# Four buffers for conditioning weights, sums transposed into a PSUM bank, and a layer norm split over two engines

## The chip, the core and the metric

The kernel runs on one core of one Trainium2 chip. The metric is device time in microseconds: the median of several executions. A profiled execution is one more run, whose trace is read below. Engines are PE (TensorE: matmuls and transposes; PEld is its weight load), DVE (VectorE), ACT (ScalarE), POOL and SP (the queue from which the weights are loaded).

## What is computed

Two blocks on x of 256 rows by 2048 columns, all in float32: a block with a gated delta rule, block attention and a feed-forward net, and then two conditioned layers. Of the second part this matters here:

```python
c_act = jax.nn.silu(c)
for l in range(2):
    mod = c_act @ w_mod[l] + b_mod[l]          # 1 x 2048 by 2048 x 6144
    shift, scale, gate = jnp.split(mod, 3, axis=-1)
    h = x * (1.0 + scale[:, None]) + shift[:, None]
    if l == 0:
        y = diff_attention(h, ...)             # products v2 k2 q2 g2, then o2
    else:
        mod = c_act @ w_mod_kv + b_mod_kv      # 1 x 2048 by 2048 x 4096
        # keys and values of the normalized x (products v3 k3), queries and gate (q3 g3), o3
        y = forgetting_attention(h, ...)
    x = layer_norm(DN_ALPHA * x + gate[:, None] * y, ln_g[l], ln_b[l])
```

The vectors `mod` depend on `c` alone, so they can be computed at any earlier time.

## The kernel before

Rows of x are the 128 partitions, in two halves `th`. Each product reads its weights in units of 256 x 512 (512 KB). A unit goes through a ring of four slots: SP loads it into `raw` (L467), ACT casts it to `w_hi` (L1281, `split`), DVE subtracts to get `w_lo` (L1908, `split`), and PE multiplies three ways: `w_hi` by the high operand, `w_lo` by the high one, `w_hi` by the low one (L661 to L663, or L686 to L688 in the transposed form). Each engine's program is written out in the order in which it runs, and the semaphores `w_landed`, `hi_done`, `lo_done` and `w_used` tie them. ACT and DVE work four units ahead: at unit j they prepare unit j + 4, ACT waits until unit j is used (`w_used`), and SP's load of unit j waits for `lo_done` of unit j - 4 (L465). A list `between(j)` hangs other work on the units.

The conditioning vectors are computed beside the products `qkv`, `spill`, `w_out`, `ffn`, `down`, `v2`, `k2` and `q2`, in 32 chunks of 512 columns. A chunk is 16 steps, one per unit: SP loads 128 x 512 of `w_mod` (256 KB) into `gemv_w[:, k % 2]` and DVE adds it, times one entry of `c_act`, to `gemv_acc` (L1924, L1927). SP issues step j - 5 right behind the weight load of unit j; the load of step k waits until step k - 2 has been added (`gemv_step`, L490), and what follows in SP's queue waits with it. After the last step DVE transposes `gemv_acc` in 32 x 32 blocks into `gemv_t` (L1931) and reduces that to `gemv_sums` (L1935); at unit 5 of the next chunk PE adds over partitions into bank `MODB` (L696), and at unit 7 ACT copies and stores the result (L1306, L1309).

Between `qkv` and `spill` lies a gate computation: DVE forms the argument of a softplus (L2096 to L2102), ACT takes Exp (L1425) and Ln (L1426), and PE, after two units of `spill` that carry nothing else and a third, waits for `softplus_log` before it goes on (L794). Its own next steps are sums of squares (L802).

The first layer's end, `o2`, is followed at once by `v3`, whose operand is the normalized x, and nothing else is left for PE between them. The last two units of `o2` run the upper rows first and then the lower (`rows_apart`, L637 to L639). DVE drains each half (L2520, L2524), takes moments (L2529, L2552), ACT takes a dummy Sqrt, which loads the table, and the root (L1786, L1333), DVE the reciprocal (L2587) and then, chunk by chunk, both halves of `normalized` (L2601), each raising `ln_out`. PE turns chunk c when `ln_out` has reached 2(c + 1) (`turn_normed`, L1222; the transposes are L604). From the turned blocks `even_block` on DVE (L2459) and `odd_block` on ACT (L1723) make the modulated operand, ACT casts it to `s_hi` (L1712), DVE subtracts `s_lo` (L2466), and PE's unit j of `v3` needs blocks j (`cut_by`). `v3` starts with the first two chunks turned and turns the third and fourth behind its units 0 and 1.

Of the kernel before, what the change touches and what calls it, by code (L numbers as in the profile page):

```python
# [18 lines left out]
F32 = mybir.dt.float32  # L19
F32R = mybir.dt.float32r  # L20
ALU = mybir.AluOpType
# [4 lines left out]
P = 128  # L26
# [13 lines left out]
SQ = 32  # L40
RING = 4
RMS_EPS = 1e-6
EPS = 1e-5
# [70 lines left out]
def block_kernel(nc, x, norm_mix_w, w_in, conv_w, a_log, dt_bias, gdn_o_norm_w, q_norm_w, k_norm_w,  # L114
# [5 lines left out]
    with ctx:  # L120
# [14 lines left out]
        keep = place("keep", [P, KEEP_W], F32)  # L135
        cols = place("cols", [P, 3 * P], F32)
        modc = place("modc", [P, P], F32)
        small = place("small", [P, 464], F32)
        stage = place("stage", [P, 2, HALVES, COLS], F32)
        f_first = place("f_first", [P, H3, P], F32, at[0])  # L140
        gemv_w = place("gemv_w", [P, 2, COLS], F32)
        gemv_acc = place("gemv_acc", [P, COLS], F32)
        gemv_t = place("gemv_t", [P, COLS], F32)
        gemv_sums = place("gemv_sums", [P, COLS // SQ], F32)
# [103 lines left out]
        def h_stage(q):  # L248
# [9 lines left out]


        SS, RR, GCOL, BB, EGL, NEGA, ALOG, DTB = 0, 32, 64, 128, 144, 176, 177, 178  # L260
        LN_STATS, LN_MOMENTS = 336, 322
        E6, E5, QNS, BFC, MX, SUM, RCP, LAM, RELB, FCOL, CACT = (
            179, 180, 181, 182, 192, 256, 320, 384, 400, 416, 448)
        c_act = small[:, CACT:CACT + KD]
# [82 lines left out]
        x_in = (sem("x_in0"), sem("x_in1"))  # L347
        gemv_landed = (sem("gemv_landed0"), sem("gemv_landed1"))
        gemv_cut = sem("gemv_cut")
# [105 lines left out]
        def _(sp):  # L455
# [23 lines left out]
            def load_gemv(pr, i, j, w, col):  # L479

                if without_mod(pr, i):
                    return
                part = pr.units // pr.mods
                m, k = j // part, j % part
                if k >= KD:
                    return
                n = mod_base(pr, i) + m
                if not (isinstance(i, int) and (n + i * pr.mods) * KD + k < 2):

                    sp.wait_ge(gemv_step, i * (pr.mods * KD) + (n * KD + k - 1))  # L490
                sp.dma_start(gemv_w[:, k % 2], w[k * P:(k + 1) * P, ds(col + m * COLS, COLS)]).then_inc(gemv_landed[k % 2], 16)

# [100 lines left out]
        def _(pe):  # L593
# [627 lines left out]
            def turn_normed(c):  # L1221
                pe.wait_ge(signal("ln_out"), HALVES * (c + 1))  # L1222

                turn_x(products["v3"], c, lambda q: (signal("h_odd"), c) if q else (signal("h_block"), 8 + c))

            turn_normed(0)
            turn_normed(1)
# [43 lines left out]
        def _(act):  # L1271
# [495 lines left out]
            def layer_tail(name, p, layer, extra=None):  # L1767
# [5 lines left out]
                if layer:  # L1773
                    ln_weights(layer)

                for i in range(pr.bodies):
                    def between(j, i=i):
                        if i == 0 and j == 3:
                            outputs_high(pr, p, 3)
                        if extra:  # L1780
                            extra(i, j)


                    body(name, i, nothing, between, finish=(lambda: None) if i == pr.bodies - 1 else None)

                own.link(act.activation(ln_tmp[layer][:, 0, D - 1:D], sm(E5, 1), ACT.Sqrt, bias=sm(E5, 1)))  # L1786
                if layer == 0:
                    act.wait_ge(signal("moments"), HALVES)
                    root(0, small[:, LN_MOMENTS + 1:LN_MOMENTS + 2 * HALVES:2], sm(RR, HALVES), 1.0, E5, "root_ln")
                    return  # L1790
                for th in range(HALVES):
                    act.wait_ge(signal("moments"), HALVES + th + 1)
                    root(0, sm(LN_MOMENTS + 2 * th + 1), sm(RR + th), 1.0, E5, "root_ln")

# [66 lines left out]

            layer_tail("o2", "d", 0, forget_weights)
            odd_block(1)
            for q in range(2):
                v3_operand(q)
            for i in range(2):
                def between(j, i=i):
                    if i == 0 and j < 3:
                        v3_operand(2 * j + 2)
                        v3_operand(2 * j + 3)  # L1870
# [30 lines left out]
        def _(dve):  # L1901
# [8 lines left out]
            def gemv(pr, i, j):  # L1910
# [7 lines left out]
                n = mod_base(pr, i) + m  # L1918
                c_k, w_k = c_act[:, k:k + 1], gemv_w[:, k % 2]
                dve.wait_ge(gemv_landed[k % 2], i * (pr.mods * 8 * KD) + (n * 8 * KD + 16 * (k // 2 + 1)))  # L1920
                if k == 0:
# [7 lines left out]
                if k == KD - 1:  # L1929
                    dve.wait_ge(gemv_step, i * (pr.mods * KD) + (n * KD + KD))  # L1930
                    dve.transpose(gemv_t[:], gemv_acc[:]).then_inc(gemv_cut, 1)  # L1931
                    dve.wait_ge(gemv_cut, i * (pr.mods * 2) + (2 * n + 1))
                    if not (isinstance(i, int) and i * pr.mods + n == 0):
                        dve.wait_ge(mod_stored, i * (pr.mods * 16) + 16 * n)
                    dve.tensor_reduce(gemv_sums[:], gemv_t[:].rearrange("p (b c) -> p b c", c=SQ), AX.X, ALU.add).then_inc(  # L1935
                        gemv_cut, 1)
# [579 lines left out]
            def residual_drain(pr, i, x, ths=range(HALVES)):  # L2516
# [5 lines left out]
                for th in ths:  # L2522
                    c = xs[:, th, ds(i * (2 * COLS) + x * COLS, COLS)]
                    dve.scalar_tensor_tensor(out=c, in0=c, scalar=ALPHA, in1=stage[:, x, th], op0=ALU.mult,  # L2524
                                             op1=ALU.add).then_inc(signal("x_mixed"), 1)
                layer, chunk = int(pr is products["o3"]), 2 * i + x
                for th in ths:
                    dve.wait_ge(signal("x_mixed"), 8 * layer + 2 * chunk + th + 1)
                    own.inc(dve.bn_stats(sm(LN_STATS + 24 * th + 6 * chunk, 6), xs[:, th, chunk * COLS:(chunk + 1) * COLS]))  # L2529
# [7 lines left out]
            def layer_tail(name, p, layer, extra=None):  # L2537
# [26 lines left out]
                def last_of_x():  # L2564
# [4 lines left out]
                    if layer:  # L2569
                        dve.wait_ge(signal("moments"), HALVES + 1)  # L2570
                        dve.wait_ge(signal("ln_in"), 64)
                        own.inc(centred(0, slice(0, D)))
                        dve.wait_ge(signal("root_ln"), 2)
                        own.link(dve.reciprocal(sm(RR), sm(RR)))
# [8 lines left out]

                if layer == 0:
                    dve.wait_ge(signal("moments"), HALVES)
                    dve.wait_ge(signal("root_ln"), 1)
                    own.link(dve.reciprocal(sm(RR, HALVES), sm(RR, HALVES)))  # L2587
                    return
                finished(0, parts[1])
                dve.wait_ge(signal("moments"), 2 * HALVES)  # L2590
                own.inc(centred(1, parts[0]))
                dve.wait_ge(signal("root_ln"), 3)
                own.link(dve.reciprocal(sm(RR + 1), sm(RR + 1)))
# [242 lines left out]
```

## Time and profile before

| | us |
|---|---|
| median of 3 runs | 2598.83 (2596.96 to 2603.57) |
| profiled execution | 2601.48 |
| its span, first to last instruction | 2599.7 |
| PE busy | 2554.0 |
| DVE busy | 1803.6 |
| ACT busy | 1154.6 |
| mean granted clock of PE | 0.995 of full speed |

All times in the rows below count from the start of the span. PE is called busy from the start of a matmul to its modelled end. The granted clock is the share of 2.4 GHz that the chip let PE run at; it has two levels, 1.00 and 0.50.

### The profile page before, as it was taken

How to read it: one execution, taken by the hardware profiler on the slowest of the kernel's cores; microseconds unless marked ns; L12 is line 12 of the kernel's file. 1: busy time of each engine (PE TensorE's matmuls, PEld its weight loads, DVE VectorE, ACT ScalarE, POOL GpSimd, SP SyncE). 2: the span in 40 equal slices, each digit the busy share in tenths (PEclk: the TensorE clock that was granted, in tenths of full speed). 3: DMA queues.
4: the chain of work that ended last, by engine and by line, in shares of the span. 5: the costliest groups of instructions: out<-in, count | busy, mean ns of one | idle time of the engine just before them, and what ended most of it. 6: DMA issues, size and time to landing. Idle time of an engine off the chain costs nothing.

```text
span 2599.7 us, 38429 instructions
## 1 busy us (share of the span) xinstructions
PE 2554.0 (98%) x14550; PEld 2156.5 (83%) x14550; DVE 1803.6 (69%) x2342; ACT 1154.6 (44%) x1475; POOL 0.2 (0%) x4
## 2 busy tenths in 40 slices
PE   8999999999999999999999999999999999999998
PEld 8977878778888888888888888899987778999886
DVE  6897676776667777777776666776786665545756
ACT  5454333445544544444443334333486344334642
POOL 0000000000000000000000000000000000000000
PEclk9999999999999999999999999999999999999999
DMA  6777676776768888888887777888845546675464
GB/s 212 247 236 247 210 249 216 255 255 211 251 227 271 270 276 276 270 272 278 277 276 250 251 253 258 280 275 275 257 138 189 186 159 181 185 230 178 137 215 143
DMA packets 317949, 605.74 MB, mean 233 GB/s; under 512 B 27742, under 2 KB 31844, under 8 KB 316140
## 3 DMA queue, kind: packets, MB, share of 16 engines
q1 hardware_dynamic: 301628, 571.59, 68.3%
q10 hardware_dynamic: 16176, 32.15, 3.6%
q8 instruction: 99, 1.62, 0.2%
q14 instruction: 46, 0.38, 0.0%
HBM read 593.03 MB, written 10.62 MB: 232 GB/s over the span
## 4 chain that ended last, share of the span: by engine, by line
PE 90%; DVE 4%; DMA 2%; ACT 2%; issue 2%; SPq 0%; ACTq 0%; DVEq 0%
PE bank L661 22%; PE bank L663 22%; PE bank L662 22%; PE bank L688 5%; PE bank L686 5%; PE bank L687 5%; DMA gemv_w<-in_w_mod 2%; PE bank L604 2%; PE bank L787 1%; DVE gemv_acc L1927 1%; DVE w_lo L1908 1%; DVE conv_out L2056 1%; ACT w_hi L1281 1%; PE bank L1120 1%; PE bank L813 0%
## 5 line engine op out<-in xcount | busy, mean ns | idle before, releaser
L1908 DVE TENSOR_TENSOR w_lo<-raw,w_hi 128x1024 fp32r<-128x1024 f32 x820 | 1001.7, 1223 | 725.9 <-ACT w_hi L1281 723.9
L1281 ACT CAST w_hi<-raw 128x1024 fp32r<-128x1024 f32 x820 | 859.3, 1049 | 1347.1 <-PE bank L663 1001.7
L661 PE MATMUL bank<-w_hi,u_hi 128*128 128x512 f32 x1216 | 491.9, 404 | 6.3 <-issue 3.8
L663 PE MATMUL bank<-w_hi,u_lo 128*128 128x512 f32 x1216 | 481.2, 396 | 0.0
L662 PE MATMUL bank<-w_lo,u_hi 128*128 128x512 f32 x1216 | 480.9, 395 | 0.0
L1927 DVE SCALAR_TENSOR_TENSOR gemv_acc<-gemv_w,small,gemv_acc 128x512 f32<-128x512 f32 x480 | 357.9, 746 | 23.2 <-DMA gemv_w<-in_w_mod 21.9
L661 PE MATMUL bank<-w_hi,s_hi 128*128 128x512 f32 x744 | 300.9, 404 | 1.3 <-DVE w_lo L1908 1.2
L663 PE MATMUL bank<-w_hi,s_lo 128*128 128x512 f32 x744 | 294.2, 395 | 0.0
L662 PE MATMUL bank<-w_lo,s_hi 128*128 128x512 f32 x744 | 294.2, 395 | 0.0
L688 PE MATMUL bank<-s_hi,w_lo 128*128 128x256 f32 x1024 | 290.1, 283 | 0.0
L687 PE MATMUL bank<-s_lo,w_hi 128*128 128x256 f32 x1024 | 289.5, 283 | 0.0
L686 PE MATMUL bank<-s_hi,w_hi 128*128 128x256 f32 x1024 | 288.7, 282 | 0.0
L661 PEld LDWEIGHTS bank<-w_hi,u_hi 128*128 128x128 f32 x1216 | 229.7, 189 | 65.6 <-issue 10.2
L663 PEld LDWEIGHTS bank<-w_hi,u_lo 128*128 128x128 f32 x1216 | 229.7, 189 | 53.9
L662 PEld LDWEIGHTS bank<-w_lo,u_hi 128*128 128x128 f32 x1216 | 230.0, 189 | 49.3
L686 PEld LDWEIGHTS bank<-s_hi,w_hi 128*128 128x128 f32 x1024 | 193.7, 189 | 0.3
L688 PEld LDWEIGHTS bank<-s_hi,w_lo 128*128 128x128 f32 x1024 | 193.1, 189 | 0.0
L687 PEld LDWEIGHTS bank<-s_lo,w_hi 128*128 128x128 f32 x1024 | 192.7, 188 | 0.1
L663 PEld LDWEIGHTS bank<-w_hi,s_lo 128*128 128x128 f32 x744 | 140.4, 189 | 33.0
L661 PEld LDWEIGHTS bank<-w_hi,s_hi 128*128 128x128 f32 x744 | 140.6, 189 | 32.7 <-DVE w_lo L1908 1.6
L662 PEld LDWEIGHTS bank<-w_lo,s_hi 128*128 128x128 f32 x744 | 140.7, 189 | 30.6
L661 PE MATMUL bank<-w_hi,hid_hi 128*128 128x512 f32 x352 | 139.8, 397 | 0.0
(362 smaller groups left out, 2882.6 us busy)
## 6 DMA issues: line engine op xcount, KB each, us to landing
gemv_w<-in_w_mod SPq DMA_DIRECT2D x384, 256.0 KB, 3.2
raw<-in_w_in SPq DMA_DIRECT2D x176, 512.0 KB, 4.5
raw<-in_a_w_in SPq DMA_DIRECT2D x128, 512.0 KB, 4.5
raw<-in_w_ffn_gate SPq DMA_DIRECT2D x88, 512.0 KB, 4.6
raw<-in_w_ffn_up SPq DMA_DIRECT2D x88, 512.0 KB, 4.4
raw<-in_w_ffn_down SPq DMA_DIRECT2D x88, 512.0 KB, 4.3
gemv_w<-in_kv_w_mod SPq DMA_DIRECT2D x128, 256.0 KB, 3.5
raw<-in_kv_w SPq DMA_DIRECT2D x64, 512.0 KB, 3.7
```

The source lines that it names most:

```text
L604: ins = pe.transpose(b[:, f * T + th * P:f * T + (th + 1) * P], src(f, th), ident)
L661: pe.matmul(o, xh, w_hi[:, s, t], start=(k == 0), stop=False)
L662: pe.matmul(o, xh, w_lo[:, s, t], start=False, stop=False)
L663: ins = pe.matmul(o, xl, w_hi[:, s, t], start=False, stop=(k == 2 * units - 1))
L686: pe.matmul(o, wh, hi[:, k], start=(k == 0 and f % 2 == 0), stop=False)
L687: pe.matmul(o, wh, lo[:, k], start=False, stop=False)
L688: ins = pe.matmul(o, wl, hi[:, k], start=False, stop=(k == 2 * half - 1 and f % 2 == 1))
L787: ins = pe.matmul(dst[rr, n:n + CHUNK], lhs[rr, th, h], rhs[rr, th, h], start=True, stop=True)
L1120: pe.matmul(b[:, P:3 * P], queries_of[p][:, a, P:T], k_t[:, a, 0:T], start=True, stop=True).then_inc(signal(p + "_scores"), 1)
L1281: act.copy(w_hi[:, s], raw[:, s]).then_inc(hi_done, 1)
L1908: dve.tensor_tensor(w_lo[:, s], raw[:, s], w_hi[:, s].bitcast(F32), ALU.subtract).then_inc(lo_done, 1)
L1927: dve.scalar_tensor_tensor(out=gemv_acc[:], in0=w_k, scalar=c_k, in1=gemv_acc[:], op0=ALU.mult, op1=ALU.add).then_inc(gemv_step, 1)
```

## The change

Three edits are made together.

1. `gemv_w` has four buffers in place of two, with a semaphore for each; the load of step k waits for step k - 4. Space comes from `gemv_t`, which goes, and from shorter `cols` and `small`.
2. DVE transposes `gemv_acc` into `bank[MODB]` and reduces from there. It waits for the store of the chunk before (`mod_stored`) ahead of the transpose, no longer between transpose and reduce.
3. In the layer norm after `o2`, ACT normalizes the upper half (`upper_normalized`: Identity with scale and a bias `SHIFTED` that DVE computes as minus mean times reciprocal root), and DVE the lower half. ACT's dummy Sqrt moves ahead of its last two casts, and the root of the upper half ahead of the last. PE runs 16 matmuls of 512 columns on the operand of the layer before, into `bank[MODB]`, between `o2` and the first transposes; nothing reads them. A semaphore `x_rows` takes over what `x_mixed` counted and, for DVE's half, what `ln_out` counted.

```diff
-        cols = place("cols", [P, 3 * P], F32)
+        cols = place("cols", [P, LN_B + KD], F32)
-        small = place("small", [P, 464], F32)
+        small = place("small", [P, 448], F32)
-        gemv_w = place("gemv_w", [P, 2, COLS], F32)
+        gemv_w = place("gemv_w", [P, GEMV_RING, COLS], F32)
-        gemv_t = place("gemv_t", [P, COLS], F32)
...
# SP, load_gemv
-                if not (isinstance(i, int) and (n + i * pr.mods) * KD + k < 2):
-                    sp.wait_ge(gemv_step, i * (pr.mods * KD) + (n * KD + k - 1))
-                sp.dma_start(gemv_w[:, k % 2], w[k * P:(k + 1) * P, ds(col + m * COLS, COLS)]).then_inc(gemv_landed[k % 2], 16)
+                if not (isinstance(i, int) and (n + i * pr.mods) * KD + k < GEMV_RING):
+                    sp.wait_ge(gemv_step, i * (pr.mods * KD) + (n * KD + k - (GEMV_RING - 1)))
+                sp.dma_start(gemv_w[:, k % GEMV_RING], w[k * P:(k + 1) * P, ds(col + m * COLS, COLS)]).then_inc(gemv_landed[k % GEMV_RING], 16)
...
# PE, before v3
             def turn_normed(c):
-                pe.wait_ge(signal("ln_out"), HALVES * (c + 1))
+                pe.wait_ge(signal("ln_out"), c + 1)
+                pe.wait_ge(signal("x_rows"), 8 + 1 + c + 1)
...
+            for n in range(16):
+                pe.matmul(bank[MODB][:], s_hi[:, n, 0:P], s_hi[:, n // 2 * 2:n // 2 * 2 + 2], start=True, stop=True)
             turn_normed(0)
...
# ACT, layer_tail
+                def first_root():
+                    own.link(act.activation(ln_tmp[layer][:, 0, D - 1:D], sm(E5, 1), ACT.Sqrt, bias=sm(E5, 1)))
+
+                def root_ln(th):
+                    act.wait_ge(signal("moments"), HALVES * layer + th + 1)
+                    root(0, sm(LN_MOMENTS + 2 * th + 1), sm(RR + th), 1.0, E5, "root_ln")
...
-                    body(name, i, nothing, between, finish=(lambda: None) if i == pr.bodies - 1 else None)
-
-                own.link(act.activation(ln_tmp[layer][:, 0, D - 1:D], sm(E5, 1), ACT.Sqrt, bias=sm(E5, 1)))
-                if layer == 0:
-                    act.wait_ge(signal("moments"), HALVES)
-                    root(0, small[:, LN_MOMENTS + 1:LN_MOMENTS + 2 * HALVES:2], sm(RR, HALVES), 1.0, E5, "root_ln")
-                    return
-                for th in range(HALVES):
-                    act.wait_ge(signal("moments"), HALVES + th + 1)
-                    root(0, sm(LN_MOMENTS + 2 * th + 1), sm(RR + th), 1.0, E5, "root_ln")
+                        if layer == 0 and i == pr.bodies - 1 and j == pr.units - 1:
+                            root_ln(0)
+                    body(name, i, nothing, between, finish=first_root if i == pr.bodies - 1 else None)
+
+                if layer:
+                    root_ln(0)
+                root_ln(1)
+
+            def upper_normalized(c):
+                act.wait_ge(signal("x_rows"), 8 + 1)
+                part = xs[:, 0, c * COLS:(c + 1) * COLS]
+                act.activation(part, part, ACT.Identity, scale=sm(RR), bias=sm(SHIFTED)).then_inc(signal("ln_out"), 1)
...
             layer_tail("o2", "d", 0, forget_weights)
+            upper_normalized(0)
+            upper_normalized(1)
             odd_block(1)
...
                 def between(j, i=i):
+                    if i == 0 and j < 2:
+                        upper_normalized(2 + j)
...
# DVE, gemv
-                    dve.transpose(gemv_t[:], gemv_acc[:]).then_inc(gemv_cut, 1)
-                    dve.wait_ge(gemv_cut, i * (pr.mods * 2) + (2 * n + 1))
                     if not (isinstance(i, int) and i * pr.mods + n == 0):
                         dve.wait_ge(mod_stored, i * (pr.mods * 16) + 16 * n)
-                    dve.tensor_reduce(gemv_sums[:], gemv_t[:].rearrange("p (b c) -> p b c", c=SQ), AX.X, ALU.add).then_inc(
+                    dve.transpose(bank[MODB][:], gemv_acc[:]).then_inc(gemv_cut, 1)
+                    dve.wait_ge(gemv_cut, i * (pr.mods * 2) + (2 * n + 1))
+                    dve.tensor_reduce(gemv_sums[:], bank[MODB][:].rearrange("p (b c) -> p b c", c=SQ), AX.X, ALU.add).then_inc(
                         gemv_cut, 1)
...
# DVE, layer_tail and normalized
-                    dve.wait_ge(signal("moments"), HALVES)
-                    dve.wait_ge(signal("root_ln"), 1)
-                    own.link(dve.reciprocal(sm(RR, HALVES), sm(RR, HALVES)))
+                    dve.wait_ge(signal("root_ln"), 1)
+                    own.link(dve.reciprocal(sm(RR), sm(RR)))
+                    dve.wait_ge(signal("moments"), HALVES)
+                    dve.scalar_tensor_tensor(out=sm(SHIFTED), in0=sm(LN_MOMENTS), scalar=-1.0, in1=sm(RR), op0=ALU.mult,
+                                             op1=ALU.mult).then_inc(signal("x_rows"), 1)
+                    dve.wait_ge(signal("root_ln"), 2)
+                    own.link(dve.reciprocal(sm(RR + 1), sm(RR + 1)))
                     return
...
             def normalized(c):
                 part = slice(c * COLS, (c + 1) * COLS)
-                for th in range(HALVES):
-                    dve.tensor_scalar(xs[:, th, part], xs[:, th, part], sm(LN_MOMENTS + 2 * th), sm(RR + th), ALU.subtract,
-                                      ALU.mult).then_inc(signal("ln_out"), 1)
+                dve.tensor_scalar(xs[:, 1, part], xs[:, 1, part], sm(LN_MOMENTS + 2), sm(RR + 1), ALU.subtract,
+                                  ALU.mult).then_inc(signal("x_rows"), 1)
```

## Rows read from the trace of the kernel before

**Rows 1.** The page: busy us by engine, share of the span, instructions.

```profile
PE 2554.0 (98%) x14550; PEld 2156.5 (83%) x14550; DVE 1803.6 (69%) x2342; ACT 1154.6 (44%) x1475; POOL 0.2 (0%) x4
```

**Rows 2.** Windows of 20 us: length, busy by engine, PE clock, DMA share, GB/s.

```profile
160.00:180.00 20.00, 15.29 (x71) 12.55 (x71) 17.52 (x26) 12.64 (x17) 0.00 (x0) 0.91 0.74 241
520.00:540.00 20.00, 19.94 (x90) 15.97 (x90) 16.75 (x17) 7.83 (x7) 0.00 (x0) 1.00 0.95 329
540.00:560.00 20.00, 17.61 (x73) 13.73 (x72) 18.77 (x18) 11.30 (x16) 0.00 (x0) 0.91 0.76 240
2080.00:2100.00 20.00, 14.64 (x62) 11.54 (x63) 14.21 (x26) 10.24 (x18) 0.00 (x0) 0.74 0.27 79
```

**Rows 3.** Waits of PE, 60 to 182 us: us in total, times, longest.

```profile
PE bank L686 <- DVE w_lo L1908: 1.8, 3, 0.9
```

**Rows 4.** Waits of DVE for conditioning weights: 100-180, 165-181, 500-540 us.

```profile
DVE gemv_acc L1927 <- DMA gemv_w<-in_w_mod: 7.5, 7, 1.9
DVE gemv_acc L1927 <- DMA gemv_w<-in_w_mod: 2.1, 2, 1.7
DVE gemv_acc L1927 <- DMA gemv_w<-in_w_mod: 4.2, 4, 2.5
```

**Rows 5.** The chain that ended last, near 525 us: start, us, what.

```profile
524.90 7.55 DMA gemv_w<-in_w_mod
```

**Rows 6.** Timeline, 160 to 181 us: start, us, engine, line, what, [idle before, releaser].

```profile
166.13 1.05 ACT L1281 CAST w_hi<-raw 128x1024 fp32r<-128x1024 f32 x1 [3.03 <-DMA raw<-in_w_in]
169.13 1.22 DVE L1908 TENSOR_TENSOR w_lo<-raw,w_hi 128x1024 fp32r<-128x1024 f32 x1
171.28 0.39 PE L663 MATMUL bank<-w_hi,u_lo 128*128 128x512 f32 x1
171.98 0.39 PE L663 MATMUL bank<-w_hi,u_lo 128*128 128x512 f32 x1
173.52 0.42 DVE L2102 TENSOR_TENSOR gates<-gates 8x256 f32<-8x256 f32 x1
175.70 0.41 ACT L1426 ACTIVATE gates<-gates 8x256 f32<-8x256 f32 x1
176.22 0.64 PE L661 MATMUL bank<-w_hi,u_hi 128*128 128x512 f32 x1 [3.85 <-issue]
179.64 0.46 PE L663 MATMUL bank<-w_hi,u_lo 128*128 128x512 f32 x1
```

**Rows 7.** Timeline, 545 to 549 us.

```profile
546.75 2.35 DVE L1908 TENSOR_TENSOR w_lo<-raw,w_hi 128x1024 fp32r<-128x1024 f32 x2
548.01 0.50 PE L661 MATMUL bank<-w_hi,u_hi 128*128 128x512 f32 x1 [2.39 <-DVE w_lo L1908]
```

**Rows 8.** Timeline of the layer norm and the start of v3, 2080 to 2097 us.

```profile
2081.64 0.30 ACT L1333 ACTIVATE small<-small 128x2 f32<-128x2 f32 x1
2082.24 1.92 DVE L2601 TENSOR_SCALAR xs<-xs,small 128x512 f32<-128x512 f32 x4
2083.34 1.94 PE L604 MATMUL bank<-keep,xs 128*128 128x128 f32 x8 [4.48 <-issue]
2087.68 0.77 PE L661 MATMUL bank<-w_hi,s_hi 128*128 128x512 f32 x1
2096.70 0.63 PE L604 MATMUL bank<-keep,xs 128*128 128x128 f32 x4 [0.71 <-DVE stage L2459]
```

**Rows 9.** Groups by form: count, busy us, mean ns of one, idle before.

```profile
L1931 DVE STREAM_TRANSPOSE gemv_t<-gemv_acc 128x512 f32<-128x512 f32 x32 | 22.8, 712 | 1.1
L2208 DVE TENSOR_REDUCE small<-work 128x1 f32<-128x256 f32 x32 | 13.1, 409 | 0.0
L2208 DVE TENSOR_REDUCE small<-bank 128x1 f32<-128x256 f32 x8 | 3.3, 413 | 0.0
L1712 ACT CAST s_hi<-stage 128x512 fp32r<-128x512 f32 x8 | 4.8, 619 | 8.3 <-DVE stage L2459 8.2
L1723 ACT ACTIVATE stage<-bank,modc 128x256 f32<-128x256 f32 x8 | 4.1, 557 | 3.4 <-PE bank L604 3.4
```

More of the change, by code:

```diff
@@ L41 @@
 RING = 4
+GEMV_RING = 4
 RMS_EPS = 1e-6
@@ L257, in block_kernel @@
         operand_of = {"d": (s_hi, s_lo), "f": (s2_hi, s2_lo)}
+        SHIFTED = 410
         SS, RR, GCOL, BB, EGL, NEGA, ALOG, DTB = 0, 32, 64, 128, 144, 176, 177, 178
@@ L262, in block_kernel @@
         E6, E5, QNS, BFC, MX, SUM, RCP, LAM, RELB, FCOL, CACT = (
-            179, 180, 181, 182, 192, 256, 320, 384, 400, 416, 448)
+            179, 180, 181, 182, 192, 256, 320, 183, 384, 416, 392)
         c_act = small[:, CACT:CACT + KD]
@@ L347, in block_kernel @@
         x_in = (sem("x_in0"), sem("x_in1"))
-        gemv_landed = (sem("gemv_landed0"), sem("gemv_landed1"))
+        gemv_landed = [sem(f"gemv_landed{s}") for s in range(GEMV_RING)]
         gemv_cut = sem("gemv_cut")
@@ L1918, in gemv @@
                 n = mod_base(pr, i) + m
-                c_k, w_k = c_act[:, k:k + 1], gemv_w[:, k % 2]
-                dve.wait_ge(gemv_landed[k % 2], i * (pr.mods * 8 * KD) + (n * 8 * KD + 16 * (k // 2 + 1)))
+                c_k, w_k = c_act[:, k:k + 1], gemv_w[:, k % GEMV_RING]
+                dve.wait_ge(gemv_landed[k % GEMV_RING], i * (pr.mods * 4 * KD) + (n * 4 * KD + 16 * (k // GEMV_RING + 1)))
                 if k == 0:
@@ L2524, in residual_drain @@
                     dve.scalar_tensor_tensor(out=c, in0=c, scalar=ALPHA, in1=stage[:, x, th], op0=ALU.mult,
-                                             op1=ALU.add).then_inc(signal("x_mixed"), 1)
+                                             op1=ALU.add).then_inc(signal("x_rows"), 1)
                 layer, chunk = int(pr is products["o3"]), 2 * i + x
                 for th in ths:
-                    dve.wait_ge(signal("x_mixed"), 8 * layer + 2 * chunk + th + 1)
+                    dve.wait_ge(signal("x_rows"), 13 * layer + 2 * chunk + th + 1)
                     own.inc(dve.bn_stats(sm(LN_STATS + 24 * th + 6 * chunk, 6), xs[:, th, chunk * COLS:(chunk + 1) * COLS]))
@@ L2572, in last_of_x @@
                         own.inc(centred(0, slice(0, D)))
-                        dve.wait_ge(signal("root_ln"), 2)
+                        dve.wait_ge(signal("root_ln"), 3)
                         own.link(dve.reciprocal(sm(RR), sm(RR)))
@@ L2591, in layer_tail @@
                 own.inc(centred(1, parts[0]))
-                dve.wait_ge(signal("root_ln"), 3)
+                dve.wait_ge(signal("root_ln"), 4)
                 own.link(dve.reciprocal(sm(RR + 1), sm(RR + 1)))
```

## The prediction

> **What bounds the kernel now.** The first view is busy time by engine: TensorE (PE) works 2554.0 of 2599.7 us [rows 1]. Only the 45.7 us in which it stands still, and the stretches in which its clock is low, can be won; work saved on another engine counts for nothing unless PE waits for it. The second view, PE and clock in slices of 20 us, shows where that is: 4.7 us idle from 160 to 180 and 2.4 from 540 to 560, both with a mean clock of 0.91, and 5.4 from 2080 to 2100 with 0.74 [rows 2]. The rest lies at the start and the end of the span and in pieces of about 1 us that no edit touches, but for three waits for the low half of the weights, 1.8 us in all, between 60 and 182 [rows 3].
>
> Then each hole is read. VectorE (DVE) waited 7.5 us for conditioning weights between 100 and 180, 2.1 of that after 165, and 4.2 between 500 and 540 [rows 4]. The chain that ended last runs through such loads: a 256 KB load that took 7.55 us stands on it [rows 5]. The reason is in the code: with two buffers the load for step k waits until step k-2 has been added up, and the sync queue (SP) holds the next weight load behind that wait.
>
> At 172 us PE has finished three units and waits for softplus_log. The order is visible: DVE's last w_lo split at 169.13, then gemv, transpose, reduce, the gate arithmetic with its last step at 173.52, then ScalarE (ACT) with Exp, a table load and Ln, done at 176.11; PE starts again at 176.22 after 3.85 idle, and its next 8 intervals take 3.42 us, 0.43 each, against 0.23 before [rows 6]. That is the 1.2 GHz level in place of 2.4. At 548.01 PE had waited 2.39 us for a split that DVE began at 546.75 [rows 7]. In the third hole PE stops at 2078.87, the layer norm runs alone on DVE, and PE's transposes start at 2083.34, after 4.48 us, at 1.2 GHz (8 in 1.94 us); the first matmul of v3 starts at 2087.68, and the transposes of the last chunk wait again until 2096.70 [rows 8].
>
> **The change, part by part.**
> *Four buffers, first hole.* SP's wait for the load of step k now asks for step k-4, which is done before the split that frees the raw buffer next in the queue. The conditioning load leaves about one unit (2.8 us) sooner and the weight load behind it about one gemv sooner, so DVE's waits of up to 2.5 us go. How early can DVE be? At least 2.1 (the waits after 165). At most 5.9: the w_lo of a unit needs its w_hi, which needs the unit four before it used; three units of 12 matmuls at 0.233 ended at 172.37, so that one was used at 164.0 and, with the three small waits gone, at 162.2, so w_hi ends at 163.2 (1.05 long) where DVE started at 169.13 [rows 3, 6]. I take the middle, 4.0. The gate arithmetic then ends at 169.9 instead of 173.9; ACT's 2.2 us behind it stay; softplus_log comes at 172.1. PE reaches the wait 1.8 earlier, at 170.6, stands 1.5 us, and goes on 4.0 us earlier than before. After waits of up to 0.9 [rows 3] the clock stayed (the 0.09 that the slice from 160 lost is 3.4 us at half speed, all of it after 176), after 2.39 and more it fell [rows 2, 7]; I count 1.5 with the former, so the slow matmuls, 8 x (0.4275 - 0.233) = 1.56 us, are saved too. Term: 5.6. Bounds: 2.1 (least shift, clock falls) and 7.2 (no idle left: 1.8 + 3.85 + 1.56). DVE waits for less and nothing new is queued ahead of it; what is late next is ACT's Exp, table load and Ln.
>
> *Second hole.* The gemv waits in 500 to 540 are 4.2 us and the missing time is 2.39, so the split comes in time and PE keeps its clock: 2.39 + 1.56 = 4.0. Bounds: 4.0 and 0, if the weight loads, in a stretch whose DMA engines are 95% busy [rows 2], arrive no sooner. I take 4.0, since the waits exceed what is missing by 1.8 us.
>
> *Elsewhere* DVE's waits for these loads end no wait of PE: its own are those of rows 3 and 6 to 8 and the pieces of 1 us. 0.
>
> *Transpose into a bank.* A transpose of 128x512 into SBUF takes 0.711 us; none into a bank is in the trace. The nearest row is the reduce of 128x256, 0.413 from a bank and 0.409 from SBUF [rows 9]. So 0 to 0.01 per chunk on DVE, in both directions; bound from above 0.1, the whole being covered by DVE's slack except for four chunks at the two holes: 0 taken, 0.4 at most. The wait for mod_stored moves ahead of the transpose; that store is issued at unit 7 of a group and the transpose stands at unit 15, some 22 us later, so nobody waits; behind it would stand the next split.
> The Trainium skill (Perfetto Trace Analysis, section Optimizing Scalar/DVE Operations) gives DVE about 60 ns of access time on SBUF and 125 ns on a bank. By it transpose and reduce would cost 0.13 us more per chunk, as an estimate 0.5 us for the four chunks that matter, and the sum would be 11.2. The two reduce rows show 4 ns, and I go by them.
>
> *Layer norm on two engines, 16 matmuls on PE.* Before, DVE makes four passes in 1.92 us from 2082.24, and PE starts after two of them [rows 8]. Now ACT takes the upper half's pass while DVE takes the lower. ACT's 128x512 pass with scale and bias is not in the trace: 0.62 for a plain one is the lower bound, and 0.56 for 256 columns with scale and bias [rows 9], doubled, 1.1 the upper. I take 0.75, nearer to the row of the same size. The dummy Sqrt and its table load move from just ahead of the root, which ran from 2081.64 [rows 8], to ahead of ACT's last two w_hi casts, where ACT waits for PE anyway; I count 0.2 for that. ACT's pass needs one small DVE step more (the shift) but not the lower half's reciprocal, 0.2 again. So it starts about 0.4 before 2082.24 and both halves of chunk 0 are ready at about 2082.6, against 2083.3. The 16 matmuls (16 x 0.233 = 3.7 from 2078.9) end at 2082.6, as that chunk gets ready, and cost PE nothing; the clock is then high for the transposes (8 in about 1.0 instead of 1.94). First matmul of v3: before 2087.68, now about 2086.3 (0.7 from the norm, 0.6 from faster transposes). It runs full speed, but the end of the stretch is set by DVE and ACT: unit 0 used, w_hi, w_lo, one normalizing pass (0.5 shorter than two), the even block, then the transposes that waited until 2096.70. This moves from 2096.70 to about 2094.5. Term: 2.1. Bounds: 2.4, and 1.0 if ACT's pass takes 1.1, three times in its queue ahead of a copy that DVE waits for. If the clock falls all the same in the gaps left between transposes and unit 0, unit 0 ends 1.6 later, which that second wait swallows but for 0.3.
> The same page and section of the Trainium skill says that where DVE has a faster mode an operation is quicker there, which speaks against moving a pass to ACT. The trace agrees: 0.48 a pass on DVE (four in 1.92) against 0.62 at least on ACT [rows 8, 9]. By it one chunk would be ready after 0.96 on DVE alone, after 0.75 on both: only 0.2 us of this term come from the second engine.
>
> Sum: 5.6 + 4.0 + 2.1 = 11.7. The profiled execution took 2601.48 us (span 2599.7 and 1.8 around it): 2589.8. The median before, 2598.83, is 2.65 lower, perhaps because a clock that fell here doesn't fall in every run; then less is to be won. From the median 11.7 gives 2587.1. I say **2588.0**.
>
> **Rivals.**
> *The weight loads become the wait.* ACT waited 3.03 us at 166.13 for a raw weight load [rows 6]; if these loads land no sooner, DVE waits for w_hi instead of gemv_w. Gain 2.1 in the first hole, 0 in the second, 2.1 in the layer norm: 2594.6. For it: the 95% in rows 2. Against: the raw loads leave sooner too.
> *It moves nothing.* The holes are filled by other waits at once (softplus through ACT, sq_b through ACT) and ACT's passes eat the layer norm's gain: 2598. Against: the named waits are longer than what follows them.
> *Slower: the loads overtake.* In every stretch with conditioning work a unit needs 768 KB in its 12 matmuls, 2.8 us: 281 GB/s. Two more 256 KB loads in flight take their share ahead of raw weights. If this makes a unit's data take more than the 2.81 us that PE needs for it, PE waits in each of 480 units; at 0.02 us a unit that is 9.6 us with no gain: 2608. Against: 329 GB/s were moved in 520 to 540 [rows 2].
>
> **How the numbers follow.** The forecast, with its terms near 5.6, 4.0 and 2.1, gets 0.69 (2584.5 to 2591); raw loads 0.22 (2594.6); nothing 0.05 (2598); slower 0.04 (2608). The range of 8 in 10 reaches from all upper bounds (13.6 off the median, 2585.2, less 1 for the spread) into the raw-load rival: 2584 to 2595. About 0.3%, 7.8 us, is what a measurement of this kernel can tell from no change. Below 2591.0 lie the forecast and little else: faster 0.69, within 0.27, slower 0.04.
>
> **What would show it.** Right: no DVE wait for gemv_w over 0.3 us in 100 to 180 and 500 to 540; PE's wait for softplus under 1.6 us and clock 1.00 in both; 16 matmuls from 2079 on end before the transposes start, and those take about 1.0 us for 8; the last chunk's transposes come about 15.6 us after o2's last matmul instead of 17.8. Wrong: a wait of DVE for w_hi with ACT waiting for raw loads of the same length, PE idle at the softplus gate of 3 us or more, a transpose over 0.8 us, or an ACT pass over 1 us.

## The result and the profile after

The changed kernel takes 2603.2 us (median of 14 runs, 2600.61 to 2606.96), the kernel before on the same chip 2599.85 us: a ratio of 1.0015, 95% interval 1.0008 to 1.0022. It is slower by a hair, where 2588.0 us was forecast. The profiled execution took 2603.11 us, its span is 2601.3 us.

The page after, busy us by engine, as in [rows 1]:

```profile
PE 2567.8 (99%) x14566; PEld 2159.7 (83%) x14566; DVE 1799.9 (69%) x2340; ACT 1157.8 (45%) x1480; POOL 0.2 (0%) x4
```

PE stood still for 2601.3 - 2567.8 = 33.5 us, against 45.7 before: 12.2 us less idle time. But PE was *busy* for 13.8 us more. The 16 extra matmuls are 3.8 of that; the other 10.0 come although the matmuls behind the three holes no longer run at the low clock.

Windows of 20 us after, with the columns of [rows 2]:

```profile
160.00:180.00 20.00, 19.88 (x94) 14.48 (x93) 18.88 (x31) 17.03 (x22) 0.00 (x0) 1.00 0.78 257
540.00:560.00 20.00, 20.00 (x94) 16.38 (x95) 17.08 (x16) 11.13 (x15) 0.00 (x0) 1.00 0.81 254
2080.00:2100.00 20.00, 16.83 (x86) 12.86 (x85) 15.20 (x27) 12.50 (x20) 0.00 (x0) 1.00 0.28 79
2460.00:2480.00 20.00, 18.12 (x93) 15.05 (x92) 11.06 (x26) 12.41 (x23) 0.00 (x0) 0.91 0.41 124
```

The three holes read as intended. At 160 PE works 19.88 us instead of 15.29 and at 540 all 20.00 instead of 17.61, both with the clock at 1.00. At the layer norm, 2080 to 2100, it is 16.83 instead of 14.64 (3.8 of it the extra matmuls) with the clock at 1.00 instead of 0.74. One clock fall is new, near 2470, where PE waits 1.88 us for ACT; the kernel before has a wait of 1.9 us at this place, and its clock stays at 1.00.

DVE's waits for conditioning weights, 100 to 180 and 500 to 540 us, as in [rows 4]: in total, times, longest:

```profile
DVE gemv_acc L1947 <- DMA gemv_w<-in_w_mod: 0.3, 1, 0.3
DVE gemv_acc L1947 <- DMA gemv_w<-in_w_mod: 1.1, 1, 1.1
```

From 7.5 to 0.3 us, and from 4.2 to 1.1. The end of the gate computation, start and length as in [rows 6]:

```profile
168.25 0.42 DVE L2122 TENSOR_TENSOR gates<-gates 8x256 f32<-8x256 f32 x1
170.43 0.41 ACT L1430 ACTIVATE gates<-gates 8x256 f32<-8x256 f32 x1
```

DVE's last gate step begins at 168.25, 5.3 us before its counterpart in [rows 6], and Ln is done at 170.84. PE has finished its three units at 170.83 and goes on at 170.94, so it hardly stops for it any more. The layer norm after, against [rows 8]:

```profile
2079.70 3.81 PE L1229 MATMUL bank<-s_hi 128*128 128x512 f32 x16
2082.08 0.26 DVE L2572 BATCH_NORM_AGGREGATE small<-small 128x2 f32<-128x24 f32 x1
2082.38 0.29 ACT L1337 ACTIVATE small<-small 128x1 f32<-128x1 f32 x1 [1.37 <-DVE small L2572]
2082.64 1.52 ACT L1809 ACTIVATE xs<-xs,small 128x512 f32<-128x512 f32 x2
2082.90 1.00 DVE L2624 TENSOR_SCALAR xs<-xs,small 128x512 f32<-128x512 f32 x2
2083.55 1.06 PE L605 MATMUL bank<-keep,xs 128*128 128x128 f32 x8
2087.05 0.47 PE L662 MATMUL bank<-w_hi,s_hi 128*128 128x512 f32 x1 [0.62 <-issue]
2094.94 0.63 PE L605 MATMUL bank<-keep,xs 128*128 128x128 f32 x4 [0.85 <-DVE stage L2479]
```

PE's 16 matmuls end at 2083.51, both engines' first passes (ACT's two take 1.52 us, DVE's two 1.00) are through by then, and 8 transposes take 1.06 us instead of 1.94. The groups that bear on [rows 9], with the same columns: the transpose and the reduce, now in a bank, and ACT's normalizing pass, which had no row before (first line: the reduce of the kernel before, from SBUF):

```profile
L1935 DVE TENSOR_REDUCE gemv_sums<-gemv_t 128x16 f32<-128x512 f32 x32 | 22.0, 686 | 2.2
L1953 DVE STREAM_TRANSPOSE bank<-gemv_acc 128x512 f32<-128x512 f32 x32 | 23.3, 727 | 2.3
L1955 DVE TENSOR_REDUCE gemv_sums<-bank 128x16 f32<-128x512 f32 x32 | 22.1, 691 | 1.1
L1809 ACT ACTIVATE xs<-xs,small 128x512 f32<-128x512 f32 x4 | 3.2, 812 | 0.0
```

So the named waits are gone but for small remainders. Where did some 15 us go, 11.7 that were forecast and 3.35 by which the kernel is slower? To a place that none of these views shows. Windows of PE alone in three long stretches without any hole: length, busy (its instructions), clock, DMA share, GB/s. First the kernel before, then the changed kernel. The first window lies in `ffn` (512 columns a matmul), the other two in `k2`/`q2` and `k3`/`q3` (256 columns):

```profile
900.00:1300.00 400.00, 400.00 (x1760) 1.00 0.85 275
1720.00:1820.00 100.00, 100.00 (x843) 1.00 0.86 276
2220.00:2320.00 100.00, 100.00 (x835) 1.00 0.68 213
```

```profile
900.00:1300.00 400.00, 400.00 (x1748) 1.00 0.86 273
1720.00:1820.00 100.00, 100.00 (x834) 1.00 0.87 273
2220.00:2320.00 100.00, 100.00 (x835) 1.00 0.69 215
```

PE is busy without a gap and at full clock in both, yet it gets through 1748 matmuls in 400 us instead of 1760, and 834 instead of 843 in 100 us. (The counts take in short ones too: of the 1760, 64 are transposes and 18 are sums of conditioning chunks. So 400 us over the count is less than the spacing of the long ones.) Loads are the same (275 and 273 GB/s). From the starts in the trace, consecutive matmuls of equal width stand 234.3 ns apart in `ffn` where it was 232.5, and 120.0 in `k2` where it was 118.7; in `k3` both have 120.0. Lining up the same matmul in both traces, the changed kernel loses 0.2 us in every 18 us of `qkv`, `k2` and `q2` and 0.24 in every 34 us of a 512-column stage. The whole account, in us: this slow drift +15.2; `qkv` and the gate (100 to 170) -8.0; the second hole -4.3; the layer norm -2.7; the clock fall ahead of `o3` near 2470 +1.6; the start +0.4. That is +2.2; the span shows 1.6 of it, since PE's first instruction came 0.6 earlier.

### The profile page after: what moved, and what is told of

It is laid out like the page before. It is cut to its first block, busy times and chain, and to the rows that moved or that the text cites. A ratio compares the mean times of both kernels' runs of the same rounds, so it can differ in the third digit from the quotient of the medians.

```text
span 2601.3 us, 38411 instructions
## 1 busy us (share of the span) xinstructions
PE 2567.8 (99%) x14566; PEld 2159.7 (83%) x14566; DVE 1799.9 (69%) x2340; ACT 1157.8 (45%) x1480; POOL 0.2 (0%) x4
## 4 chain that ended last, share of the span: by engine, by line
PE 95%; DVE 2%; ACT 2%; issue 1%; DMA 1%; ACTq 0%; SPq 0%; DVEq 0%
PE bank L662 23%; PE bank L664 22%; PE bank L663 22%; PE bank L689 7%; PE bank L687 7%; PE bank L688 6%; PE bank L605 1%; PE bank L788 1%; ACT w_hi L1285 1%; PE bank L1121 1%; DVE w_lo L1928 0%; DMA gemv_w<-in_w_mod 0%; PE bank L814 0%; PE bank L1130 0%; PE bank L803 0%
## 5 line engine op out<-in xcount | busy, mean ns | idle before, releaser
L662 PEld LDWEIGHTS bank<-w_hi,u_hi 128*128 128x128 f32 x1216 | 228.9, 188 | 60.6 <-issue 6.1
```

The source lines that it names most:

```text
L662: pe.matmul(o, xh, w_hi[:, s, t], start=(k == 0), stop=False)
```

## The experiments

What could slow a PE that never waits? Theory A: the addresses. The change makes some tiles shorter and others longer, and so moves all operands (`u_hi`, `s_hi` and the rest of the region behind `region`) from byte 104192 to 105952 of a partition, while `w_hi` stays at 32896 (`w_lo` lies 16384 behind it). The distance, operands' byte minus weights' byte, so goes from 71296 to 73056; divided by 256 these leave 128 and 96, which is what "distance modulo 256" means below. Rival B: what the change does beside PE (loads that are earlier and denser, DVE's transposes into a bank) disturbs PE.

### e1 to e4: addresses alone

e1, the changed kernel, 32 bytes lower from the staging on:

```diff
-        SHIFTED = 410
+        SHIFTED = 188
-            179, 180, 181, 182, 192, 256, 320, 183, 384, 416, 392)
+            179, 180, 181, 182, 192, 256, 320, 183, 384, 408, 392)
-        small = place("small", [P, 448], F32)
+        small = place("small", [P, 440], F32)
```

> The changed kernel with its small-vector tile 32 bytes shorter, so that everything placed behind it (staging, conditioning weights, and the region with the operands u and s) lies 32 bytes lower; nothing else differs. In the changed kernel those addresses are odd multiples of 32 bytes, here multiples of 64, as in the kernel before. Theory A (the start address of PE's operands sets how closely its matmuls follow one another: 234.3 ns for 512 columns and 120.0 ns for 256 in the changed kernel, 232.4 and 118.7 in the kernel before): the old pace returns, the 15 us that the slower pace adds along the kernel go, and the holes stay closed: 2588 us, ratio about 0.995. Rival B (the earlier and denser conditioning loads, or VectorE's transposes into the bank, slow PE): nothing moves, 2603 us, ratio 1.0015, and 234.3 and 120.0 ns stay.

2590.27 us, ratio 0.9969 [0.9959, 0.9978]. The matmuls stand 233.3 ns apart in `ffn` and 117.8 in the 256-column stages, so the pace changed, though not to that of the kernel before. The windows of e1, as above:

```profile
900.00:1300.00 400.00, 400.00 (x1754) 1.00 0.87 272
1720.00:1820.00 100.00, 100.00 (x849) 1.00 0.87 277
2220.00:2320.00 100.00, 100.00 (x851) 1.00 0.70 219
```

e2, the kernel before with 32 bytes more, and e3, with 64:

```diff
-        cols = place("cols", [P, 3 * P], F32)
+        cols = place("cols", [P, 3 * P + 8], F32)      # e2
+        cols = place("cols", [P, 3 * P + 16], F32)     # e3
```

> The kernel before with 32 bytes of padding in the column tile, ahead of the small vectors, the staging, the conditioning weights and the operands; no instruction differs. Theory A: the pace becomes that of the changed kernel (234.3 and 120.0 ns), with all holes still there: about 2600 + 15 = 2615 us, ratio 1.006. Rival B: 2600 us, ratio 1.000, the pace stays 232.4 and 118.7 ns.

2603.06 us, ratio 1.0013 [1.0004, 1.0022]: slower, but not by 15 us. 233.4 ns in `ffn`, 117.3 to 118.7 by turns for 256 columns.

> The kernel before with 64 bytes of padding at the same place. Theory A with a grain of 64 bytes: 2600 us, ratio 1.000, pace 232.4 and 118.7 ns. Theory A with a coarser grain (128 bytes or more): slower, up to 2615 us. Rival C (any shift at all disturbs the pace, by the distance of the operands from the weights or by chance): slower, like the shift of 32 bytes. Rival B: 2600 us.

2564.38 us, ratio 0.9867 [0.9852, 0.9882]. Nothing but 64 unused bytes makes the kernel before 1.3% faster, three times what the change was to bring. The windows of e3:

```profile
900.00:1300.00 400.00, 400.00 (x1789) 1.00 0.86 279
1720.00:1820.00 100.00, 100.00 (x881) 1.00 0.90 290
2220.00:2320.00 100.00, 100.00 (x851) 1.00 0.68 218
```

1789 matmuls where there were 1760, and 881 where there were 843: 228.9 and 113.4 ns; in `k3`/`q3` it is 117.8.

e4, the changed kernel with staging and conditioning buffers moved as in e1 but the operand region put back:

```diff
(the edits of e1, and)
+        at[0] += 32
         region = at[0]
```

> The changed kernel with the staging and the conditioning buffers 32 bytes lower, on multiples of 64, and 32 bytes of padding behind them, so that the operand region stays where the changed kernel has it. Theory A, by the operands of the matmuls: nothing moves, 2603 us, ratio 1.0015, 234.3 and 120.0 ns. Theory A', by the buffers that VectorE, ScalarE and the DMAs write beside PE (staging, conditioning weights): 2588 us. Rival B: 2603 us.

2604.21 us, ratio 1.0019 [1.0010, 1.0028], and the changed kernel's pace to a tenth of a ns in every stage:

```profile
900.00:1300.00 400.00, 400.00 (x1747) 1.00 0.87 272
1720.00:1820.00 100.00, 100.00 (x834) 1.00 0.86 272
```

So it is the address of the operand region, and not that of the buffers which DVE, ACT and the loads write. Rival B falls with e1 to e4: the pace changes in kernels whose instructions are the same one for one, and does not change where only the other buffers move. That the grain would be 64 bytes was wrong: 32 and 64 bytes give two different new paces.

### e5 to e8: own address or distance to the weights?

e5 moves every tile of the kernel before by 64 bytes, weights included; e8 moves the weights and keeps the operands; e6 puts the changed kernel's operands at another address with e3's distance; e7 pads 128 bytes.

```diff
-        at = [16512]
+        at = [16512 + 64]                                             # e5
-        gemv_row = place("gemv_row", [P, SQ], F32)
+        gemv_row = modc[:, 96:96 + SQ]                                # e6, with the edits of e1
+        cols = place("cols", [P, 3 * P + 32], F32)                    # e7
+        at[0] += 64                                                   # e8, ahead of w_hi
+        cols = place("cols", [P, 3 * P - 16], F32)                    # e8
```

> The kernel before with its first tile, and so every tile, 64 bytes higher: the operands u and s lie where the kernel with 64 bytes of padding has them, but the weights w_hi and w_lo move along, so the distance between operands and weights is that of the kernel before. Theory A1 (the pace goes by the operands' own address): 2564 us and 228.9 ns for a 512-column matmul in ffn, as with 64 bytes of padding. Theory A2 (it goes by the distance between operands and weights): 2599 us, 232.4 ns.

2598.26 us, ratio 0.9998 [0.9989, 1.0008], and the pace of the kernel before in every stage (matmuls begun in `ffn` and in `k2`/`q2`):

```profile
900.00:1300.00 400.00, 400.00 (x1760) 1.00 0.85 275
1720.00:1820.00 100.00, 100.00 (x843) 1.00 0.86 276
```

> The changed kernel with its operand region 160 bytes lower, at byte 105792 (the small-vector tile 32 bytes shorter, the conditioning row kept in unused columns of the modulation tile). Modulo 256 the operands then lie at 64, and 192 from the weights, as in the kernel before with 64 bytes of padding. Theory A with a grain of 256 bytes (A1 and A2 alike): that kernel's pace (228.9 ns in ffn) with the changed kernel's closed holes: 2564 - 12 = 2552 us, ratio about 0.982. Theory A3 (the pace goes by the whole address, or by chance): no reason for that pace; somewhere between 2588 and 2603 us.

2553.17 us, ratio 0.9819 [0.9806, 0.9832], at the pace of e3:

```profile
900.00:1300.00 400.00, 400.00 (x1789) 1.00 0.88 279
1720.00:1820.00 100.00, 100.00 (x882) 1.00 0.90 289
```

Its first hole is not closed in the profiled execution, which was the longest of the five (2557.81): PE comes to the gate sooner, waits 2.2 us for Ln, and its clock falls (columns of [rows 2]):

```profile
160.00:180.00 20.00, 17.82 (x75) 13.45 (x73) 19.11 (x30) 14.15 (x18) 0.00 (x0) 0.91 0.82 271
```

> The kernel before with 128 bytes of padding in the column tile. Theory A with a grain of 128 bytes: as the kernel before, 2599 us and 232.4 ns in ffn. With a grain of 256 bytes: a pace of its own, between 228.9 and 234.3 ns in ffn, 2564 to 2615 us. Rival B (contention by loads and VectorE): 2599 us.

2566.88 us, ratio 0.9881 [0.9866, 0.9897]. A pace of its own, 227.0 ns for 512 columns but 120.0 for 256:

```profile
900.00:1300.00 400.00, 400.00 (x1805) 1.00 0.86 281
1720.00:1820.00 100.00, 100.00 (x833) 1.00 0.86 273
```

> The kernel before with w_hi, w_lo, xs and the constants 64 bytes higher and the column tile 64 bytes shorter, so that the operand region stays at its address and the distance to the weights is 64 bytes less (64 modulo 256, as in the changed kernel with 32 bytes less). Theory A1 (the operands' own address): 2599 us, 232.4 ns in ffn. Theory A2 (the distance): 233.3 ns in ffn and 117.8 ns for 256 columns, about 2600 us in all, as these two shifts nearly cancel over the kernel.

2600.24 us, ratio 1.0000 [0.9991, 1.0009], at 233.3 and 117.8 ns, which is e1's pace stage by stage:

```profile
900.00:1300.00 400.00, 400.00 (x1755) 1.00 0.85 273
1720.00:1820.00 100.00, 100.00 (x849) 1.00 0.87 279
```

The four agree on theory A2: what counts is the distance between operands and weights, modulo 256 bytes. e5 keeps it and keeps the pace although every address moved. e8 changes it to that of e1 and gets e1's pace with other addresses. e6 has e3's distance at an address 1536 bytes away, and e3's pace. The full distances of e1 and e8 differ by 1792, which is a multiple of 256 but not of 512, so the pace repeats with 256 bytes. No run has the kernel before at distance 96, where the changed kernel stands; at 64 (e1, e8) and at 192 (e3, e6) the kernels with and without the change have the same pace.

### e11 and e12: the two distances left

The edit is that of e2 and e3, with `+ 40` (160 bytes) in e11 and `+ 24` (96 bytes) in e12.

> The kernel before with 160 bytes of padding in the column tile: operands 32 from the weights modulo 256, a distance not measured yet. Distances so far: 0 gives 227.0 ns for 512 columns and 119.9 for 256; 64 gives 233.3 and 117.8; 96 gives 234.3 and 120.0; 128 gives 232.4 and 118.7; 160 gives 233.4 and 117.8; 192 gives 228.9 and 113.4 to 117.7. If the slow distances lie together (64 to 160) and the quick ones around 0: between 227 and 233 ns, 2564 to 2600 us. Chance by distance: anything in 2564 to 2615 us.

2595.40 us, ratio 0.9987 [0.9977, 0.9996]; 233.3 ns, and for 256 columns 116.7 or 117.8 by turns.

> The kernel before with 96 bytes of padding in the column tile: operands 224 from the weights modulo 256, between the two quick distances 192 (228.9 ns) and 0 (227.0 ns). If the quick distances lie together: 227 to 229 ns in ffn, 2560 to 2570 us. If every 32 bytes is a law of its own: anything in 2564 to 2615 us.

2602.46 us, ratio 1.0012 [1.0003, 1.0022]; 233.3 and 118.3 ns. So the quick distances do not lie together: that expectation missed in both.

| distance mod 256, bytes | kernels | ns, 512 columns (`ffn`) | ns, 256 columns (`k2`, `q2`) | ns, 256 columns (`k3`, `q3`) |
|---|---|---|---|---|
| 0 | e7 | 227.0 | 120.0 | 120.0 |
| 32 | e11 | 233.3 | 117.3 | 116.7 |
| 64 | e1, e8 | 233.3 | 117.8 | 117.8 |
| 96 | after, e4 | 234.3 | 120.0 | 120.0 |
| 128 | before, e5 | 232.5 | 118.7 | 120.0 |
| 160 | e2 | 233.4 | 118.2 | 117.3 |
| 192 | e3, e6 | 228.9 | 113.4 | 117.8 |
| 224 | e12 | 233.3 | 118.3 | 118.3 |

The columns are means over the three windows above. With 512 columns the operand is the stationary side of the matmul and the weights move; with 256 it is the other way round, so width and role change together in this table. The changed kernel happens to stand at the slowest row. In `k3`/`q3` it loses nothing against the kernel before, since both run at 120.0.

### e9 and e10: what the two halves of the change bring at one pace

Both stand at distance 192, as e3 and e6, so that only the change itself differs. e9 is e6 without the loop `for n in range(16): pe.matmul(bank[MODB][:], ...)`; e10 has only the hunks of the diff with the four buffers and the transpose into the bank.

> The kernel before with only the first half of the change (four conditioning buffers, sums transposed into the accumulator bank) and the operand region at byte 105792 (192 from the weights modulo 256); the layer norm is that of the kernel before. The prediction's terms: 2553 us with both halves, the layer norm worth 2.1 us, so 2555 us here, and 9.6 us under the 2564 us of the kernel before at the same distance. Rival (the buffers bring less than the two holes, as PE falls into the next wait): 2558 us or more.

2554.63 us, ratio 0.9829 [0.9815, 0.9842]: 9.75 us under e3's median, where the two terms were 9.6. Lined up with e3, e10 gains 2.7 us ahead of the gate, where e3 has three waits of 2.4 us in all, 3.6 at the gate and 3.7 at the second hole. Elsewhere it gains 0.8 near 670, where e3 waits 0.73 us for a split, and 0.9 around the layer norm, where its clock recovers sooner, and loses 1.6 ahead of `o3`, where its clock falls and e3's does not; between these places the two run apart by 0.13 us from 780 to 1340 and by less than 0.03 from there to 2020. The layer norm itself is as before; PE's transposes start 4.48 us after `o2` ended, and those of the last chunk 12.7 us behind them:

```profile
2043.62 1.94 PE L605 MATMUL bank<-keep,xs 128*128 128x128 f32 x8 [4.48 <-issue]
2056.30 0.63 PE L605 MATMUL bank<-keep,xs 128*128 128x128 f32 x4 [0.98 <-DVE stage L2460]
```

> The changed kernel at byte 105792 (operands 192 bytes from the weights modulo 256) without the 16 extra matmuls ahead of v3's transposes; the layer norm stays split over two engines. The 16 write a bank that nobody reads before it is written anew, so the result is the same. Theory: they hold TensorE's clock, without them it falls to half in the layer norm as in the kernel before, and the work behind runs longer: 1 to 3 us slower than the 2553 us with them. Rival: the transposes wait for the layer norm in both, and the matmuls fill idle time only: 2553 us, at most 0.5 us off.

2553.26 us, ratio 0.9824 [0.9811, 0.9837], as e6 within its interval: the loss of 1 to 3 us that was expected did not come. In the trace the 16 matmuls do something: without them the first 8 transposes take 1.42 us and the next 1.94, and the last chunk is turned 16.2 us after `o2`'s end, where e6 has 15.2 and e10 17.2. The time does not show it:

```profile
2042.96 1.42 PE L605 MATMUL bank<-keep,xs 128*128 128x128 f32 x8 [3.85 <-ACT xs L1807]
2055.34 0.63 PE L605 MATMUL bank<-keep,xs 128*128 128x128 f32 x4 [0.29 <-DVE stage L2477]
```

### e13 and e14: one stage's operands alone

In e13 only the operands of `ffn` and `down` in e6 move, to distance 0; in e14 that of `w_out` as well.

```diff
-        u2_hi = slot("u2_hi", 0, [P, KD, T], F32R)
+        u2_hi = slot("u2_hi", 0, [P, KD, T], F32R, extra=64)
(the same for u2_lo, hid_hi, hid_lo; mod_rows makes room; e14: mix_hi, mix_lo too)
```

> The changed kernel at byte 105792 (operands 192 from the weights modulo 256) with the operands of ffn and down alone 64 bytes higher, so at distance 0. Theory A4 (each stage's pace goes by its own operands' distance): ffn and down at 227.0 ns for 512 columns as at distance 0, all other stages at the pace of distance 192; over some 755 us of these two stages that is 0.85% or 6.4 us: 2547 us, ratio 0.980. Rival A5 (one state of the whole layout, or of what ran before): ffn and down stay at 228.9 ns, 2553 us, or other stages change too.

2547.2 us, ratio 0.9805 [0.9792, 0.9818]:

```profile
900.00:1300.00 400.00, 400.00 (x1805) 1.00 0.88 281
1720.00:1820.00 100.00, 100.00 (x882) 1.00 0.90 289
```

1805 matmuls in `ffn`, e7's number, and 882 in `k2`/`q2`, e6's number. Lined up with e6, e13 gains 6.65 us between 790 and 1600, evenly, and nothing by pace anywhere else. Theory A4 holds for these stages: their pace goes by their own operands' distance, not by a state of the whole layout.

> The same with w_out's operand (mix) at distance 0 as well. Theory A4: w_out's stage, some 100 us, goes from 229 to 227 ns too: another 0.9 us, 2546 us. Rival A5: 2553 us, or no different from moving ffn and down alone by more than w_out can give.

2545.14 us, ratio 0.9795 [0.9782, 0.9809]. Lined up with e13, it gains 0.7 us between 700 and 880, as expected of `w_out`; the median's 2 us are within the spread. This is the quickest version that was run, 2.05% under the kernel before; of that about 0.4% is the change and the rest is where tiles lie.

## Why the prediction was wrong, step by step

**The step that failed** is the first one: that only the 45.7 us in which PE stands still, and the stretches with a low clock, can be won. It takes the other 2554.0 us for given, and the parts of the change were then costed by their instructions and waits alone. But the diff also changes the sizes of `cols`, `small`, `gemv_w` and `gemv_t`, and with them the place of every operand: the distance to the weights goes from 128 to 96 modulo 256. That term was not in the sum at all; it measures +15.2 us in the lined-up traces, and e1, where 32 bytes are taken back, runs 12.9 us quicker than the changed kernel (in the two measurements the kernel before differs by 1.0). A change of 0.8 to 1.1% in the matmuls' spacing is invisible in every view of idle time, because PE is never idle in it.

**Four buffers, first hole**: right. DVE ended the gate 5.3 us earlier (4.0 was taken, 5.9 the bound), softplus_log came at 170.84 (172.1) and the clock stayed. That PE met it without the stop of 1.5 us that was forecast is in part luck: Ln came 1.3 us sooner than forecast, but the slower pace also held PE back until 170.83. In quicker layouts PE is there sooner and does stop, 1.2 us in e10 and 1.4 in e1, where the clock stays at 1.00, and 2.2 in e6, where it falls to a mean of 0.91 in the slice. 5.6 was forecast, 1.8 of it from the small waits of [rows 3]; e10 against e3 gives 6.3, with 2.7 from ahead of the gate.

**Second hole**: right, 4.0 forecast, 3.7 in e10 and 4.3 in the changed kernel. A wait of DVE of 1.1 us is left there, over the 0.3 that was to be the sign; e10's PE still waits 0.83 us for a split at 535.51, with the clock at 1.00.

**Elsewhere 0**: as far as waits go, right in the changed kernel; in e10 the 0.8 near 670 are the exception.

**Transpose into a bank**: right. 727 ns against 712 [rows 9], and the reduce 691 against 686 from SBUF before: 20 ns a chunk, where 0 to 10 was taken and 100 the bound. By the Trainium skill (Perfetto Trace Analysis, section Optimizing Scalar/DVE Operations), which gives DVE about 60 ns of access on SBUF and 125 on PSUM, the two together would cost some 130 ns more, as an estimate; the measurement decides.

**Layer norm**: the end was right, the way there less so. The last chunk's transposes come 15.2 us after `o2`'s last matmul (15.6 forecast, 17.8 before); the stretch is worth 2.7 us in the lined-up traces against a term of 2.1. The same stretch gives 2.9 for e1 against e8 and 1.2 for e6 against e3; e5 against the kernel before, with the same instructions in both, gives 0.9 there, so the term is known to about 1 us only. ACT's pass is 812 ns (0.75 taken). Both halves of the first chunk are ready 3.7 us after `o2`'s end, as forecast. In the medians this half shows as 1.5 us (e10 against e6), which is within their intervals, and the 16 matmuls as nothing (e9). The clock falls at other places in some runs and not in others (ahead of `o3` in the changed kernel, e2, e5 and e10, not in the kernel before or e3, which have the same wait there), at 1.6 us each; that is as large as what is to be told apart, and it stays open.

**The sum**: 11.7 us forecast. At equal pace the whole change measures 11.2 us (e6 against e3, distance 192) and 10.0 us (e1 against e8, distance 64), by medians of runs on two chips; each ratio is known to 0.1% (2 to 4 us), so both agree with 11.7 but can't tell it from 9. The mechanism held and the sum agrees; the term that was left out was larger than the sum and had the other sign.

**The rivals**: none of the three named this. Loads that overtake were the rival on the slower side, at 2608; the traffic did not rise (273 GB/s against 275), and PE did not wait in those stretches. The Trainium skill (SBUF — State Buffer, section SBUF: two separate sides) says that transfers and engines reach this memory by separate ports and cannot contend. The runs fit it: e10 has the changed kernel's loads and transposes into the bank at e3's pace, 228.9 ns. What is left points to PE's two operands.

**What stays open** is why. No run shows how the distance acts. With 256 columns, one distance has more than one level: the kernel before runs `k2` and `q2` at 118.7 ns and `k3` and `q3` at 120.0; in e3 `k2` and `q2` run at 113.4 ns, `k3` at 113.3 until 2186, where PE puts in two short matmuls, and at 117.8 from there on, and `qkv` at 117.8, at 113.3 from a break of 0.53 us near 129 to one of 0.33 us near 153, and at 117.8 again. So PE can go over from one level to another, sometimes at a break, and a distance seems to set which levels there are. That was seen in the starts but not tested.

## What to carry over

Where PE is busy 98% of the time, compare the starts of the same matmul in two traces before reading any wait: a steady drift is not a stall, and only such a comparison shows it, or a count of matmuls over a long stretch without a stop. A change that alters the size of any tile ahead of the operands is two changes; hold the distance between stationary and moving operands fixed (pad) to measure the first, and scan it in steps of 32 bytes to see what the second is worth, stage by stage.

## What was not expected of the hardware

- In this kernel the spacing of back-to-back matmuls at full clock goes with the distance between their two operands in a partition, modulo 256 bytes: 227.0 to 234.3 ns for 512 columns (3.2%), and for 256 columns 113.4 to 120.0 in `k2`/`q2` (5.8%) and 116.7 to 120.0 in `k3`/`q3`. The quickest distance was 0 for 512 columns, 192 in `k2`/`q2` and 32 in `k3`/`q3`: for 256 columns the distance alone does not fix the pace.
- 64 unused bytes made this kernel 1.33% faster (e3); the change with all its edits gives about 0.4% at equal pace.
- Two kernels at the same distance keep step to 0.02 us over 1000 us in some pairs (e5 and the kernel before, e6 and e10), and drift by 0.1 to 0.2 in others (e10 and e3, e4 and the changed kernel), so that a gain of 0.3 us at one place can be read off lined-up traces when the times of whole runs differ by 5 us.
